# Paired attention maps in row groups, an earlier convolution norm and gains ahead of the roots, in one two-block transformer kernel

## The reference

```
def diff_attention(q1, q2, k1, k2, v, lam):      # 6 heads of 64, values of 128, blocks of 128 queries
    mask = (key_chunk[None, :] <= q_chunk[:, None])          # chunks of 64 keys
    s1 = einsum(a1, k1) * scale;  s2 = einsum(a2, k2) * scale
    p = softmax(where(mask, s1, -inf)) - lam * softmax(where(mask, s2, -inf))
    return einsum(p, v)

def _conformer_conv(val, gate, ...):
    y = depthwise_conv(val * sigmoid(gate)) + conv_b         # 31 taps, 512 channels
    return silu(_layernorm(y, ln_g, ln_b))                   # mean and variance over the channels

# second block, twice: h = h + _rmsnorm(y, g)                # the post norms
    h = h + _rmsnorm(y, g_post_mix);   f_in = _rmsnorm(h, g_pre_ffn)
    h = h + _rmsnorm(f, g_post_ffn)                          # the kernel's last work
```

## Time and profile before

| | us |
|---|---|
| median of 3 runs | 1845.86 |
| lowest, highest | 1845.82, 1846.69 |
| profiled execution | 1844.53 |
| its span | 1842.7 |
| PE busy | 1797.3 (98%) |
| DVE busy | 959.7 (52%) |
| ACT busy | 748.4 (41%) |

### The profile page before, as it was taken

How to read it: one execution, slowest core, us unless ns; L and a number is a source line. 1 busy time by engine, 2 the same in 40 slices (tenths; PEclk the granted TensorE clock), 3 DMA queues, 4 the chain that set the end, 5 groups by cost and what they waited for, 6 DMA issues and landing times.

```text
span 1842.7 us, 21548 instructions
## 1 busy us (share of the span) xinstructions
PE 1797.3 (98%) x8447; PEld 1473.4 (80%) x8447; DVE 959.7 (52%) x1724; ACT 748.4 (41%) x1471; POOL 104.8 (6%) x151
## 2 busy tenths in 40 slices
PE   8999999999999999999999999999998999999997
PEld 7887888888887777777888888888787788888886
DVE  6666443434344666755433444479986544244345
ACT  7333432323234656654232323342767432223233
POOL 0000010101011111001010101000000000000000
PEclk9999999999999999999999999999999999999999
DMA  7222233233333211112333333323100333333321
GB/s 252 80 70 85 76 108 98 93 100 94 98 96 85 68 47 58 46 47 80 94 100 94 99 95 97 98 81 103 46 12 1 92 103 98 97 95 100 102 93 57
DMA packets 195748, 158.37 MB, mean 86 GB/s; under 512 B 5248, under 2 KB 161152, under 8 KB 195648
## 3 DMA queue, kind: packets, MB, share of 16 engines
q1 hardware_dynamic: 194240, 154.16, 27.6%
q0 software_dynamic: 400, 1.25, 0.3%
q10 hardware_dynamic: 1008, 1.59, 0.2%
HBM read 154.88 MB, written 2.10 MB: 85 GB/s over the span
## 4 chain that ended last, share of the span: by engine, by line
PE 91%; DVE 5%; ACT 2%; issue 1%; DMA 0%; SPq 0%; ACTq 0%; DVEq 0%
PE ps L737 29%; PE ps L739 28%; PE ps L738 28%; PE ps L1165 1%; PE ps L789 1%; PE ps L1053 0%; DVE sb L2416 0%; DVE sb L1869 0%; PE ps L1059 0%; DVE sb L1841 0%; PE ps L848 0%; DVE sb L1843 0%; PE ps L1029 0%; DVE sb L2421 0%; ACT sb L1389 0%
## 5 line engine op out<-in xcount | busy, mean ns | idle before, releaser
L737 PE MATMUL ps<-sb,sb 128*128 128x512 f32 (+2 forms) x2547 | 984.5, 389 | 3.5 <-issue 2.4
L739 PE MATMUL ps<-sb,sb 128*128 128x512 f32 (+2 forms) x2547 | 963.6, 380 | 0.0
L738 PE MATMUL ps<-sb,sb 128*128 128x512 f32 (+2 forms) x2547 | 963.3, 380 | 0.0
L737 PEld LDWEIGHTS ps<-sb,sb 128*128 128x128 f32 x2547 | 476.5, 188 | 109.4 <-issue 14.4
L739 PEld LDWEIGHTS ps<-sb,sb 128*128 128x128 f32 x2547 | 476.3, 188 | 91.7
L738 PEld LDWEIGHTS ps<-sb,sb 128*128 128x128 f32 x2547 | 476.9, 188 | 85.6
L1843 DVE TENSOR_TENSOR sb<-sb,sb 128x512 fp32r<-128x512 f32 x532 | 348.6, 695 | 343.1 <-ACT sb L1370 342.2
L1370 ACT ACTIVATE sb<-sb 128x512 fp32r<-128x512 f32 x532 | 305.9, 623 | 432.3 <-PE ps L739 430.1
L2058 DVE TENSOR_TENSOR sb<-sb,sb 128x512 fp32r<-128x512 f32 x64 | 68.1, 1064 | 176.9 <-ACT sb L1519 176.3
L1529 ACT ACTIVATE sb<-ps 128x512 f32<-128x512 f32 x64 | 38.3, 598 | 208.6 <-PE ps L739 208.6
L665 POOL TENSOR_TENSOR sb<-sb 128x512 f32<-128x512 f32 x64 | 66.8, 1043 | 785.6 <-ACT sb L1529 785.6
(11 more groups left out here) (207 smaller groups left out, 992.0 us busy)
## 6 DMA issues: line engine op xcount, KB each, us to landing
sb<-in_w_up SPq DMA_DIRECT2D x86, 512.0 KB, 3.9
sb<-in_w_down SPq DMA_DIRECT2D x86, 512.0 KB, 3.9
sb<-in_w_gate SPq DMA_DIRECT2D x22, 512.0 KB, 3.8
sb<-in_a_w_in SPq DMA_DIRECT2D x20, 512.0 KB, 3.8
sb<-in_w_in SPq DMA_DIRECT2D x20, 512.0 KB, 3.7
sb<-in_w_o SPq DMA_DIRECT2D x16, 512.0 KB, 3.9
sb<-in_w_mem_kv SPq DMA_DIRECT2D x8, 512.0 KB, 7.7
sb<-in_w_out SPq DMA_DIRECT2D x8, 512.0 KB, 3.9
```

What stands on the lines that cost most here:

```text
L737: mm(ps, lh, rh, start=start, stop=False, **k)
L738: mm(ps, lh, rl, start=False, stop=False, **k)
L739: return mm(ps, ll, rh, start=False, stop=stop, **k)
```

## The change

The change has three parts.

**The maps of layer 1's attention in pairs.** ACT now writes the rows of queries and keys head by head (both maps of head 0, then of head 1, and so on), and copies the memory queries apart from them first (four more instructions, counter `rows_m`). After the transposes map w of every head lies in partitions 64w to 64w + 63, and its logits always go to bank `lb + w`. The mask was a matmul of 128 rows behind each map; it is now a matmul of 64 rows for each map, both behind the two maps. D waits for both exponents of the unit before it in every case, where it waited for one or none of them in some. DVE always takes two maxima (one over both maps before, where i < 2). V(g, 0), the six matmuls of 256 columns, goes from behind the piece of the next slot to the slot of D with i = 0, ahead of `sums` and D.

**The convolution's norm.** `ln_sub` goes from the end of head 6's steps to behind bt(5), `ln_dv` from head 7's steps into head 6's, the squares `ln_q` behind pt(1), and the list's end is written in another order.

**The post norms.** The gain is multiplied in ahead of the root (`post_mul`, a two-operand product), and `post_add` multiplies by the root and adds X in one instruction. PE's first four rounds of transposes for the FFN wait for the halves that they read.

```diff
 # PLAN_B
+        if s >= 4 and s % 4 == 0 and s <= 24:
+            PLAN_B[p].append(("V", s // 4 - 1, 0))
         if s >= 8 and s % 4 == 0:
             PLAN_B[p].append(("sums", s // 4 - 2))
...
-        if 0 <= s - 3 < 24 and s % 2 == 0:
-            PLAN_B[p + 1].append(("V", (s - 3) // 4, (s - 3) % 4 // 2))
+        if s >= 6 and s % 4 == 2:
+            PLAN_B[p + 1].append(("V", s // 4 - 1, 1))
 # PLAN_C, the loop over u
-        if u == 7:
-            PLAN_C += [("ln_dv",)]
         if u >= 4:
             PLAN_C += [("pt" if u % 2 else "ps", u // 2 - 2)]
...
+        if u == 7:
+            PLAN_C += [("ln_q", j) for j in range(4)]
         if u >= 1:
             PLAN_C += [("bt", u - 1)]
+        if u == 6:
+            PLAN_C += [("ln_sub",)]
...
+        if u == 6:
+            PLAN_C += [("ln_dv",)]
         if u == 7:
-            PLAN_C += [("ln_q", 0), ("ln_q", 1)]
-        PLAN_C += [("sl", u)]
+            PLAN_C += [("ln_qa", 1), ("ln_qa", 2)]
+        PLAN_C += [("taps", 2), ("sl", u)]
 # PE, turn
-                q.wait_ge(*x_ready(job, t))
+                if job == "pre_ffn" and k < 4:
+                    q.wait_ge(S("post_dve"), 2 * t + 1)
+                else:
+                    q.wait_ge(*x_ready(job, t))
 # PE, D
-                r = slice(64 * (h % 2), 64 * (h % 2) + 64)
...
-                if i == 0 and u >= 8:
-                    q.wait_ge(S("df_exp"), 2 * u - 1)
-                    head_sums(u // 4 - 2)
+                q.wait_ge(S("df_exp"), 2 * u)
+                if i == 0 and u >= 8:
+                    head_sums(u // 4 - 2)
                 for w in range(2):
-                    q.wait_ge(S("df_exp"), (2 * u - 1, 2 * u - 2, 2 * u - 2 + 2 * w, 2 * u - 1 + w)[i])
-                    b, c0 = logits_at(i, w)
-                    tl = h // 2 + n // 2 * w
-                    mm3(banks[b][:, c0:c0 + nk], Qh[r, tl, 128 * i:128 * i + 128], Ql[r, tl, 128 * i:128 * i + 128],
-                        Kh[r, tl, 0:nk], Kl[r, tl, 0:nk], True, False)
-                    m = mm(banks[b][:, c0 + nk - 128:c0 + nk], IDB[:, :], CHB[:, :], start=False, stop=True)
+                    r = slice(64 * w, 64 * w + 64)
+                    mm3(banks[B.lb + w][:, 0:nk], Qh[r, h, 128 * i:128 * i + 128], Ql[r, h, 128 * i:128 * i + 128],
+                        Kh[r, h, 0:nk], Kl[r, h, 0:nk], True, False)
+                for w in range(2):
+                    r = slice(64 * w, 64 * w + 64)
+                    m = mm(banks[B.lb + w][:, nk - 128:nk], MQ[r, :], MK[r, :], start=False, stop=True)
 # ACT, ev
+                if buf == "QB":
+                    act(QB[:, t, 256:512], banks[4 + t][:, 256:512], ACT.Copy, scale=r).then_inc(S("rows_m"), 1)
-                act(ROWS[buf][:, t, :], banks[4 + t][:, 0:n], ACT.Copy, scale=r).then_inc(S("rows"), 1)
+                act(ROWS[buf][:, t, 0:128 * h].rearrange("p (h w d) -> p w h d", w=2, h=h),
+                    banks[4 + t][:, 0:128 * h].rearrange("p (w h d) -> p w h d", w=2, h=h), ACT.Copy, scale=r).then_inc(
+                    S("rows"), 1)
 # DVE, D: the two maxima for every i; post norms:
-            stt(TF[:, t, o], src, FS[:, 8 + t:9 + t], GP[:, o], ALU.mult, ALU.mult).then_inc(S("post_v"), 1)
+            tt(TF[:, t, o], src, GP[:, o], ALU.mult).then_inc(S("post_v"), 1)
...
-            tt(X[:, t, o], TF[:, t, o], X[:, t, o], ALU.add).then_inc(S("post_dve"), 1)
+            stt(X[:, t, o], TF[:, t, o], FS[:, 8 + t:9 + t], X[:, t, o], ALU.mult, ALU.add).then_inc(S("post_dve"), 1)
...
         for t in range(4):
-            post_b(1, t)
-            post_mul(1, t, 0)
-            post_add(1, t, 0)
+            post_a(1, t)
+            post_mul(1, t, 1)
             if t < 3:
-                post_a(1, t + 1)
-            post_mul(1, t, 1)
-            post_add(1, t, 1)
-            if t < 2:
-                last_sum(t + 2)
+                last_sum(t + 1)
+            post_b(1, t)
+            for h in range(2):
+                post_add(1, t, h)
+            if t < 3:
+                post_mul(1, t + 1, 0)
```

More of the change, by code:

```diff
@@ L164, in build @@
     MEMX = place([128, 2, D], F32, r_off + 3072 + 4096)
-    CT = place([128, 512], F32, a_off + 30720)
+    CT = place([128, 384], F32, a_off + 30720)
     slabs = []
@@ L392, in build @@
         PLAN_C += [("taps", 5)]
-    BEHIND = [("tile", x) for x in IN_LATER] + [("cv", g) for g in range(3)] + [("ln_sub",), ("none",)]
+    BEHIND = [("tile", x) for x in IN_LATER] + [("cv", g) for g in range(3)] + [("none",)] * 2
     for u in range(8):
@@ L446, in build @@
     assert PAIR_NORMS == [("pair", s[1]) if s[0] == "pr" else ("ln",) for s in PLAN_C if s[0] in ("pr", "ln_rs")]
-    IN_7 = [s for s in PLAN_C if s[0] in ("cv", "pt", "ln_sub", "ln_var", "ln_mul") or s[0] == "tile" and s[1] in IN_LATER]
+    IN_7 = [s for s in PLAN_C if s[0] in ("cv", "pt", "ln_sub", "ln_var") or s == ("ln_mul", 0) or s[0] == "tile" and s[1] in IN_LATER]
     class Mem:
@@ L826, in mem_step @@
                 else:
-                    q.wait_ge(S("rows"), a[0] + 1)
+                    q.wait_ge(S("rows_m"), a[0] + 1)
                 for pr in range(2):
@@ L1027, in unit_step @@
                 q.wait_ge(S("roped"), 2 * B.rope[buf, t] + 2)
-                for j in range(2 if buf == "QB" else WIDE[buf] // 2):
-                    m = e.transpose(banks[B.tb][:, 128 * j:128 * j + 128], ROWS[buf][:, t, 128 * j:128 * j + 128], IDENT)
+                n = 2 if buf in ("QB", "KB") else 4
+                for h in range(n):
+                    m = e.transpose(banks[B.tb][:, 128 * h:128 * h + 128], ROWS[buf][:, t, 128 * h:128 * h + 128], IDENT)
                 m.then_inc(S("mb_b6"), 1)
@@ L1234, in block_step @@
                 m.then_inc(S("ln_ps"), 1)
-            elif kind == "ln_mul":
+            elif step == ("ln_mul", 0):
                 q.wait_ge(S("rs_n"), 3 * USE["ln",] + 3)
@@ L1621, in unit_step @@
                 for w, E in ((0, E1[:, u % 3, 0:nk]), (1, E2[:, u % 2, 0:nk])):
-                    b, c0 = logits_at(i, w)
-                    act(E, banks[b][:, c0:c0 + nk], ACT.Exp, bias=M[:, 2 + w:3 + w], scale=r[:, w:w + 1],
+                    act(E, banks[B.lb + w][:, 0:nk], ACT.Exp, bias=M[:, 2 + w:3 + w], scale=r[:, w:w + 1],
                         accum_out=M[:, 4 + w:5 + w]).then_inc(S("df_exp"), 1)
@@ L2370, in block_step @@
             elif kind == "ln_qa":
-                for j in range(1, 4):
-                    q.wait_ge(S("ln_q"), j + 3)
-                    tt(GL[:, 0, 0:T], GL[:, j, 0:T], GL[:, 0, 0:T], ALU.add).then_inc(S("ln_q"), 1)
+                q.wait_ge(S("ln_q"), a[0] + 3)
+                tt(GL[:, 0, 0:T], GL[:, a[0], 0:T], GL[:, 0, 0:T], ALU.add).then_inc(S("ln_q"), 1)
             elif kind == "ln_var":
@@ L2378, in block_step @@
                 rsqrt_b(("ln",), LNR, 4)
-            elif kind == "ln_mul":
+            elif kind == "ln_mul" and a[0] == 1:
                 q.wait_ge(S("ln_ps"), 3)
@@ L2420, in post_add @@
             q.wait_ge(S("post_v"), 8 * c + 2 * t + h + 1)
-            tt(X[:, t, o], TF[:, t, o], X[:, t, o], ALU.add).then_inc(S("post_dve"), 1)
+            stt(X[:, t, o], TF[:, t, o], FS[:, 8 + t:9 + t], X[:, t, o], ALU.mult, ALU.add).then_inc(S("post_dve"), 1)
         POST_A = [5, 7, 9, 11]
         POST_B = [6, 8, 10, 12]
-        post_a(0, 0)
         for t in range(4):
+            post_mul(0, t, 0)
+            post_a(0, t)
+            post_mul(0, t, 1)
             post_b(0, t)
             for h in range(2):
-                post_mul(0, t, h)
-            for h in range(2):
                 post_add(0, t, h)
-            if t < 3:
-                post_a(0, t + 1)
         weights(SL["gt", 0] + 1)
```

71 lines of the change are left out of this document (36 added, 35 removed).

## The result

| us | before | changed |
|---|---|---|
| median of 5 runs | 1845.86 | 1829.27 |
| lowest, highest | 1844.83, 1847.12 | 1825.36, 1830.39, and one of 2003.72 |
| span of the profiled execution | 1842.7 | 1825.6 |
| profiled execution | 1844.53 | 1827.43 |

The ratio is 0.9901 with a 95% interval of 0.9888 to 0.9913: faster, by 16.6 us between the medians. The run of 2003.72 us was disturbed (its mean granted clock was 0.845), the ratio leaves it out, and the median of the other four is 1828.35, 17.5 us under before. Forecast were 1825.2, with a range of 1816 to 1837. Run again beside other kernels (e9), the changed kernel had 1828.44, all but the same, and a ratio of 0.9892 (0.9875 to 0.9908): there the kernel before had 1849.71, 21.3 us more. The median of the kernel before was between 1845.16 and 1849.71 in the four sessions; why is not shown.

A forecast was written before the change was run, and what follows sets the result against it. PE was taken as the bound, busy 1797.3 of 1842.7 us. Gains of 12.6 (part one) + 6.4 (part two) + 0.45 + 1.2 (part three) = 20.7 us, subtracted from the median, gave 1825.2, range 1816 to 1837.

The forecast's parts named there:

- What bounds the kernel, and where a change can gain: Whole kernel: PE idles only 45 us, so gains come from less PE work or from removing one of its few waits.
- D's lengths: Layer 1's attention: paired maps shorten D to 0.55, 0.63 and 0.96 us for i = 0, 1, 3, saving 19.7 us.
- The waits behind i = 0: Layer 1's attention, before D with i = 1: new waits for exponents, 1.84 and three of 1.31, together 5.8 us lost.
- The other waits, 1.8 us: Layer 1's attention: second maximum, further copies, QA and KA waits, step from i = 3 to 0; 1.8 us lost, bounds 0, 6.
- V(5, 0), 0.5 us gained: End of layer 1's attention: V(5, 0) fills 0.5 us of the old wait ahead of the last sums.
- Second block: Waits at pt(1), bt(7), `ln_mul` and half clock go, a 2.55 us wait at bt(7) comes: 6.4 us gained, bounds 2.3, 8.9.
- First post norm: PE starts FFN rounds after the first half, but the shortened wait returns behind ACT's copies: 0.45 us gained, bounds 0, 1.3.
- The end: DVE's last stretch: two of eight products (t = 0) move ahead into idle time, 1.2 us gained, bounds 0 and 2.
- Serial maps: Layer 1's attention, D: maps do not run side by side, part one gains 0, total 1837; chance 0.11.
- Slower clock behind new waits: Five new waits lower the clock, costing up to 15 us: 1833 if half do, 1840 if all; chance 0.10.
- More than forecast: Shorter exponent waits give 4 us more, bt(7) without wait 2.5: 1818; chance 0.08.
- Slower than before: D's wait for both exponents, 1.0 us longer on average at all 24 units, costs 24 us: 1849 or more; chance 0.05.

The follow-up runs named there:

- e9: The changed kernel once more, unaltered, for a second profile beside other kernels: 1828.44 us, ratio to before 0.9892.
- e4: Changed kernel with both maps of a head in the same 64 partitions as before, the rest of part one kept: 1836.76 us, ratio to before 0.9952.
- e5: Changed kernel with V's places as before, V(g, 0) behind the piece after D with i = 0, V(5, 0) too: 1829.12 us, ratio to before 0.9908.
- e10: Changed kernel with, on DVE, the step's work ahead of the weights' remainders in slots with KA's transposes: 1827.53 us, ratio to before 0.9885.
- e2: Kernel before with part two alone, the convolution's norm (ln_sub, ln_dv, squares, list's end): ratio to before 0.9970, 5.8 us by medians.
- e6: Changed kernel with ACT's exponents at i = 0 of heads 2 to 5 ahead of the preceding scaling and the weight rounding: 1831.45 us, ratio to before 0.9922.
- e7: Changed kernel with e6's ACT order and V(g, 0) behind D with i = 0 for g = 0 to 4: 1828.71 us, ratio to before 0.9906.

## Why the prediction was right, point by point

**What bounds the kernel, and where a change can gain:** right. What was gained is less work on PE and four waits that went or shrank.

**D's lengths:** right to 0.02 us, but for one D (head 0, i = 3) with a wait of T inside it. Forecast 0.55, 0.63, 0.88 saved of 1.67 (so 0.79) and 0.96; measured 0.56, 0.63, 0.80 and 0.98. The basis, the memory attention's pairs, was the right one, and the rule of the Trainium skill ("TensorE: Matmul & The Clock Gate", Part 3, What overlaps and what doesn't) that matmuls start strictly in program order did not hold for D either: all three matmuls of map 0 stand ahead of those of map 1 in the program, and the rows list them as pairs (L736 twice, then L737 twice, then L738 twice). That also limits what is said ahead of the prediction, that an engine does its instructions strictly in the order of the plan. e4 shows that it is the layout that does it: with both maps in one row group the six take 0.80 us for i = 1, in two groups 0.46 (from 771.26 to the first mask).

**The waits behind i = 0:** right. Forecast 1.84 and three times 1.31, measured 1.66, 1.21, 1.19, 1.20 (three of them, and their 5.2 us in the table, just under the signs named, 1.3 to 1.8 and 6 to 9). I had taken them for the price of V's move; e5 shows that V's place makes no difference to the time, as the step before is as tight.

**The other waits, 1.8 us: the term that was mis-sized.** Between the Ds 9.4 us were added, and 0.6 inside one of them; without the 5.3 of the exponents that leaves 4.7 where 1.8 was forecast (bounds 0 and 6). The transposes of rows took 1.8 of it: their waits went from 2.35 to 4.2 us, most at 725.9, where DVE had its own queue and PE merely came 1.3 us earlier (e10). T took 0.6 in head 0, and i = 3 came 0.3 to 0.4 us later in heads 3 to 5, which no run isolates; the last 1.2 us are in pieces of 0.2 or less. I had checked each step against the chain alone, and not against what DVE had in its queue when all of PE's steps came sooner.

**V(5, 0), 0.5 us gained:** wrong. The rows before and now, of the last sums and of T of the last unit:

```profile
811.11 1.05 PE L1014 MATMUL ps<-sb,sb 128*128 128x2 f32 x8 [1.63 <-ACT sb L1623]
...
814.62 0.63 PE L1059 MATMUL ps<-sb,sb 128*128 128x128 f32 x4
```

```profile
802.82 1.05 PE L1019 MATMUL ps<-sb,sb 128*128 128x2 f32 x8 [0.49 <-ACT sb L1635]
...
806.33 0.63 PE L1065 MATMUL ps<-sb,sb 128*128 128x128 f32 x4 [0.67 <-DVE sb L2188]
```

V did fill the wait of the sums, 0.49 us for 1.63. But where it stood before, ahead of T, T now waits 0.67 us for DVE's difference of the maps, and PE is 8.3 us ahead in front of both and behind them: nothing was gained.

**Second block:** forecast 6.4 us, measured 6.5 in the profile and 5.8 alone. The new wait at bt(7) was 2.76 for 2.55, `ln_var` waits 0.4 that had no term, `ln_mul`'s 2.1 is gone, and the clock behind pt(1) is 1.00. The half clock had cost more than the 2.0 of the forecast: bt(6) now takes 3.06 us for 5.31, and pt(1) 0.35 to the next start for 0.77. That the 6.4 was met within 0.1 is in part luck: it needs the clock behind the new wait at bt(7) to stay at 1.00, and of eight profiles with this wait only that of the result has it so; with 4.59 us for bt(7), as in e2's profile, PE is 5.6 us ahead by this part.

**First post norm:** forecast 0.45, measured 0.4, by the mechanism named: ACT's squares stand in front of its copies, and 1.7 us taken from the waits for X came back as 2.0 in the next. ACT's first copy starts right behind its squares now, where it stood idle 0.47 us before (1467.55 before, 1452.18 now, 15.4 us sooner, with PE 14.8 ahead).

**The end:** forecast 1.2 of time behind PE's last matmul, measured 1.9 in the span and 2.2 to DVE's last instruction. The two products moved into idle time as said. What I left out: before, each product was followed by the addition that needs it, 0.78 + 0.61 us from start to start, 2.78 for two. Now two products take 0.60 to 0.61 each and the two additions 1.33 to the next start (1817.79 to 1819.12), 2.55. That is 0.9 us over the four token blocks.

**Rivals.** Serial maps: refuted by the rows and by e4. (Its own time, 1845.86 less 6.4, 0.45 and 1.2, is 1837.8, just outside the range that is said to take it in.) Slower clock behind new waits: in part true, in most profiles and not in that of the result: behind the longest wait of the key transposes (1.2 us in e9) and at bt(7) (4.59 us in e2 for the 3.33 of the earlier trace rows; 0.9 us lost in e9 and not 1.26, since `ln_var` then does not wait). Behind the four waits for the exponents no profile but e10's shows it. More than forecast: no, the chain of the exponents left 5.2 us of 5.8 and bt(7) waits. Slower than before: the exponents' waits were 5.2 us and not 24.

**The level.** The profiled execution's own account is 9.3 + 6.5 + 0.4 + 1.9 − 0.9 = 17.2 against 17.1 measured and 20.7 forecast. 3.3 of the difference is the attention's: 2.9 the other waits, 0.5 V(5, 0), 0.4 the Ds' lengths, less 0.5 for the shorter waits behind i = 0. 0.9 is the start, where PE's matmuls go over to the shorter distance at 14.5 us in this execution and at 12.5 in that of before, and which e9 did not have; the end and the second block gave 0.8 more than forecast.

## What to carry to other kernels

Before a reordering for a row-group overlap is doubted or believed, look for a place in the same program that already has it: its rows gave D's length to 0.02 us. Where PE gets faster through a long stretch with steps of other engines between, a gain on PE is paid out only as far as those engines' queues have room, so look at what they have in their queues over the same stretch and not only at the chain of one step; here half of the saved 18.7 us was taken back (9.4). Where several steps of a ring are equally tight, moving work from one wait to the next gains nothing (e5, e6, e7), and neither does filling one wait with work whose old place then waits (V(5, 0)). And one profile is one execution: before a clock of 1.00 behind a wait is called a gain, look at the same place in a second profile.

## What was not expected of the hardware

- Whether the clock falls behind a given wait differs between executions of one kernel: behind the same 2.1 us wait it read 0.50 in one profile of the changed kernel and 1.00 in the other, and 0.50 in four other kernels. Behind the 2.8 us at bt(7) the product took 3.33 us in one profile and 4.58 to 4.62 in seven.
- The two maps' matmuls start in pairs 0.01 us apart though the program lists all three of one map first (the x2 rows of D), and two maps in one row group do not (e4).
- On DVE a three-operand instruction of 128 x 512 took 0.67 us to the next start where the next did not need its result (1.33 for two, from 1817.79), and 0.78 where it did (the last product before, 1838.76 to the 1839.54 of the earlier trace rows).
- The 64-row masks of 128 columns, listed as a pair, took 0.17 us to the next transpose (780.99 to 781.16), against 0.07 from the second 128-row mask to it before (788.00 to the 788.07 of the earlier trace rows). Read as the cost of a change of shape, that is about 0.1 us, once instead of three times; no run isolates it.
